# Local attention: six output tiles with the denominator's row inside them, and the copy of queries cut in four

## The reference

```python
s = jnp.einsum('bqgrd,bkgd->bgrqk', qblk, kb) * scale      # 128 queries against 256 keys
s = jnp.where(mask, s, NEG_INF)
pr = softmax(concatenate([s, sink]))[..., :-1]
o = einsum('bgrqk,bkgd->bqgrd', pr, vb) * silu(z)
```

## Time and profile before

| what | value |
|---|---|
| median of 3 runs | 3059.87 us (3055.61 to 3060.7) |
| the profiled execution | 3053.61 us, its span 3051.8 us |
| granted TensorE clock | 0.977 of full speed |
| PE busy | 2892.7 us, 95% |
| VectorE, ScalarE, GpSimd busy | 64%, 52%, 46% |
| the local attention, from its first maxima to its last output | 476.1 to 729.3 us of the span |

### The profile page before, as it was taken

One profiled execution on the slowest core, in us unless ns is written; L12 is line 12 of the kernel. 1 busy time (PEld: TensorE's weight loads), 2 busy tenths in 40 slices (PEclk: granted clock), 3 DMA queues, 4 the chain that ended last, 5 costly groups with the idle time before them and its releaser, 6 DMA issues. The chain is left out here.

```text
span 3051.8 us, 41224 instructions
## 1 busy us (share of the span) xinstructions
PE 2892.7 (95%) x13411; PEld 2328.4 (76%) x13411; DVE 1938.8 (64%) x3398; ACT 1590.5 (52%) x2808; POOL 1392.0 (46%) x1139
## 2 busy tenths in 40 slices
PE   8999996888999999999998799999999999899998
PEld 6888884566888788777877588888888878688776
DVE  4543315663578864555664588888888887357875
ACT  3111114666445544444544277777777777534643
POOL 0022104665232540001440388888888889423353
PEclk9999997999999999999999699999999999999999
DMA  5343437565997675455799634435335342498674
GB/s 165 84 136 125 117 118 242 179 203 172 308 277 239 201 247 183 159 177 167 251 328 380 148 73 102 103 73 116 91 78 127 73 92 87 157 301 270 212 243 145
DMA packets 284760, 530.13 MB, mean 174 GB/s; under 512 B 29200, under 2 KB 110992, under 8 KB 277392
## 3 DMA queue, kind: packets, MB, share of 16 engines
q1 hardware_dynamic: 218528, 391.22, 43.3%
q10 hardware_dynamic: 66032, 136.48, 14.7%
HBM read 346.85 MB, written 180.49 MB: 173 GB/s over the span
## 5 line engine op out<-in xcount | busy, mean ns | idle before, releaser
L2609 POOL TENSOR_TENSOR mla_pl<-mla_p,mla_ph 128x512 fp32r<-128x512 f32 (+3 forms) x640 | 702.9, 1121 | 144.4 <-ACT mla_p L2458 141.5
L1523 PE MATMUL end_bank<-end_xh,end_whi 128*128 128x512 f32 x1808 | 718.1, 397 | 44.3 <-DVE end_wlo L1754 17.0
L1525 PE MATMUL end_bank<-end_xh,end_wlo 128*128 128x512 f32 x1808 | 708.2, 392 | 0.0
L1524 PE MATMUL end_bank<-end_xl,end_whi 128*128 128x512 f32 x1808 | 707.6, 391 | 0.0
L1592 ACT CAST end_whi<-early_wraw 128x1024 fp32r<-128x1024 f32 (+1 forms) x204 | 211.4, 1036 | 531.8 <-PE end_bank L1525 510.7
L2457 ACT ACTIVATE mla_ph<-mla_score 128x512 fp32r<-128x512 f32 (+3 forms) x640 | 342.4, 535 | 238.0 <-PE mla_score L2285 232.9
L1754 DVE TENSOR_TENSOR end_wlo<-early_wraw,end_whi 128x1024 fp32r<-128x1024 f32 x188 | 255.4, 1358 | 317.9 <-ACT end_whi L1592 317.7
L1523 PEld LDWEIGHTS end_bank<-end_xh,end_whi 128*128 128x128 f32 x1808 | 342.1, 189 | 134.9 <-DVE end_wlo L1754 24.6
L2542 DVE TENSOR_TENSOR mla_acc<-mla_acc,mla_p 128x512 f32<-128x512 f32 (+3 forms) x576 | 351.0, 609 | 106.6 <-ACT mla_p L2458 104.2
L1524 PEld LDWEIGHTS end_bank<-end_xl,end_whi 128*128 128x128 f32 x1808 | 342.3, 189 | 72.6 <-issue 2.9
L1525 PEld LDWEIGHTS end_bank<-end_xh,end_wlo 128*128 128x128 f32 x1808 | 341.6, 189 | 72.4
(11 more groups left out here) (242 smaller groups left out, 4985.7 us busy)
## 6 DMA issues: line engine op xcount, KB each, us to landing
early_wraw<-in_pe_gate ACTq DMA_DIRECT2D x64, 512.0 KB, 4.9
early_wraw<-in_w_out ACTq DMA_DIRECT2D x62, 512.0 KB, 7.3
early_wraw<-in_w_in ACTq DMA_DIRECT2D x56, 512.0 KB, 3.8
scratch_q<-in_rope SPq DMA_DIRECT2D x64, 256.0 KB, 2.9
swa_q<-scratch_q SPq DMA_DIRECT2D x8, 2048.0 KB, 9.2
end_factor<-scratch_inv SPq DMA_DIRECT2D x64, 256.0 KB, 9.6
scratch_proj<-end_out_f SPq DMA_DIRECT2D x64, 256.0 KB, 6.9
scratch_sum<-end_out_f SPq DMA_DIRECT2D x64, 256.0 KB, 6.3
```

Source lines behind the costliest of these rows:

```text
L1523: nc.tensor.matmul(bank, wh[:, at], xh[:, k0 + k * nq, :], start=(k == 0), stop=False)
L1524: nc.tensor.matmul(bank, wh[:, at], xl[:, k0 + k * nq, :], start=False, stop=False)
L1525: last = nc.tensor.matmul(bank, wl[:, at], xh[:, k0 + k * nq, :], start=False, stop=(k == kc - 1))
L2609: pool.tensor_tensor(p_lo[b][:, off:TC], prob[b][:, off:TC], p_hi[b][:, off:TC].bitcast(F32), ALU.subtract).then_inc(p_lo_ok, 1)
```

## The change

The number of output tiles of the local attention goes from three to six (`n_out`), and each gets 65 rows in place of 64. The row of denominators, which had three tiles of its own, now lies in row 64 of the output tile of its chunk, so the memory taken stays the same. The semaphores `stored` and `den_stored` become six each. The copy of the queries, one instruction of 64x4096 at k=5, becomes four of 64x1024 at k=9, 10, 12 and 13. Each stands at the head of VectorE's list for its step; the one at k=9 comes before the joining of the maxima. PE waits for all four before the first scores of the next unit.

```diff
+        n_out = 3 if long else 6
...
-            den_row = [s.sb(f"den_row{b}", [1, TC]) for b in range(small)]
-        o_out = [s.sb(f"o_out{b}", [HEAD_DIM, TC]) for b in range(small)]
+        o_out = [s.sb(f"o_out{b}", [HEAD_DIM if long else HEAD_DIM + 1, TC]) for b in range(n_out)]
+        if not long:
+            den_row = [tile[HEAD_DIM:HEAD_DIM + 1, :] for tile in o_out]
...
-        stored, den_stored = ([s.sem(f"{n}{b}") for b in range(small)] for n in ("stored", "den_stored"))
+        stored = [s.sem(f"stored{b}") for b in range(n_out)]
+        den_stored = [s.sem(f"den_stored{b}") for b in range(n_out)]
...
-        copy_at = 5
+        copy_at = (9, 10, 12, 13)
+        q_parts = len(copy_at)
...
-                        pe.wait_ge(q_copied, u + 1)
+                        pe.wait_ge(q_copied, q_parts * (u + 1))
...
-                if c >= small:
-                    act.wait_ge(den_stored[c % small], 16 * (c // small))
-                act.copy(den_row[c % small][:], o_ps[c % 2][HEAD_DIM:HEAD_DIM + 1, :]).then_inc(row_ok, 1)
+                if c >= n_out:
+                    act.wait_ge(den_stored[c % n_out], 16 * (c // n_out))
+                act.copy(den_row[c % n_out], o_ps[c % 2][HEAD_DIM:HEAD_DIM + 1, :]).then_inc(row_ok, 1)
...
-            def copy_queries(u):
+            def copy_queries(u, part):
+                mine = slice(part * qw // q_parts, (part + 1) * qw // q_parts)
...
-                vec.tensor_copy(q_tiles[1][u % 2][0:HEAD_DIM, :], q_tiles[0][u % 3][0:HEAD_DIM, :].bitcast(F32)
+                vec.tensor_copy(q_tiles[1][u % 2][0:HEAD_DIM, mine], q_tiles[0][u % 3][0:HEAD_DIM, mine].bitcast(F32)
...
-                if c >= small:
-                    dve.wait_ge(stored[c % small], 16 * (c // small))
+                if c >= n_out:
+                    dve.wait_ge(stored[c % n_out], 16 * (c // n_out))
...
-                    if not long and k == copy_at and u + 1 < units:
-                        copy_queries(u + 1)
+                    if not long and k in copy_at and u + 1 < units:
+                        copy_queries(u + 1, copy_at.index(k))
```

More of the change, by code:

```diff
@@ L2115, in attention_phase @@
             den_turned, den_copied, dens_stored = s.sem("den_turned"), s.sem("den_copied"), s.sem("dens_stored")
-        else:
-            den_row = [s.sb(f"den_row{b}", [1, TC]) for b in range(small)]
         gate = [s.sb(f"gate{b}", [HEAD_DIM, TC]) for b in range(n_gate)]
-        o_out = [s.sb(f"o_out{b}", [HEAD_DIM, TC]) for b in range(small)]
+        o_out = [s.sb(f"o_out{b}", [HEAD_DIM if long else HEAD_DIM + 1, TC]) for b in range(n_out)]
+        if not long:
+            den_row = [tile[HEAD_DIM:HEAD_DIM + 1, :] for tile in o_out]
         if long:
@@ L2272, in _ @@
             cfg["next_loads"](sp)
-            for b in range(small):
-                sp.wait_ge(stored[b], 16 * len(range(b, len(chunks), small)))
+            for b in range(n_out):
+                sp.wait_ge(stored[b], 16 * len(range(b, len(chunks), n_out)))
                 if not long:
-                    sp.wait_ge(den_stored[b], 16 * len(range(b, len(chunks), small)))
+                    sp.wait_ge(den_stored[b], 16 * len(range(b, len(chunks), n_out)))
             if long:
@@ L2429, in store @@
                     act.wait_ge(row_ok, c + 1)
-                    act.dma_start(cfg["den_dst"](*chunks[c]), cfg["row"](den_row[c % small])
-                                  ).then_inc(den_stored[c % small], 16)
+                    act.dma_start(cfg["den_dst"](*chunks[c]), cfg["row"](den_row[c % n_out])
+                                  ).then_inc(den_stored[c % n_out], 16)
                 act.wait_ge(gated, c + 1)
-                act.dma_start(cfg["dst"](*chunks[c]), cfg["gate"](o_out[c % small])).then_inc(stored[c % small], 16)
+                act.dma_start(cfg["dst"](*chunks[c]), cfg["gate"](o_out[c % n_out][0:HEAD_DIM, :])).then_inc(stored[c % n_out], 16)
             def load_gate(c):
@@ L2561, in out_gate @@
                 dve.wait_ge(gate_in[c % n_gate], 16 * (c // n_gate + 1))
-                if c >= small:
-                    dve.wait_ge(stored[c % small], 16 * (c // small))
-                vec.tensor_tensor(o_out[c % small][:], o_ps[c % 2][0:HEAD_DIM, :], gate[c % n_gate][:], ALU.mult
+                if c >= n_out:
+                    dve.wait_ge(stored[c % n_out], 16 * (c // n_out))
+                vec.tensor_tensor(o_out[c % n_out][0:HEAD_DIM, :], o_ps[c % 2][0:HEAD_DIM, :], gate[c % n_gate][:], ALU.mult
                                   ).then_inc(gated, 1)
@@ L2571, in _ @@
             if not long:
-                copy_queries(0)
+                for part in range(q_parts):
+                    copy_queries(0, part)
             for g in range(total + tail):
@@ L2594, in out_gate @@
                 pool.wait_ge(gate_in[c % n_gate], 16 * (c // n_gate + 1))
-                if c >= small:
-                    pool.wait_ge(stored[c % small], 16 * (c // small))
-                pool.tensor_tensor(o_out[c % small][:], o_sum[c % 2][:], gate[c % n_gate][:], ALU.mult
+                if c >= n_out:
+                    pool.wait_ge(stored[c % n_out], 16 * (c // n_out))
+                pool.tensor_tensor(o_out[c % n_out][0:HEAD_DIM, :], o_sum[c % 2][:], gate[c % n_gate][:], ALU.mult
                                    ).then_inc(gated, 1)
```

## The result

| | before | after |
|---|---|---|
| median of 4 runs (lowest to highest), us | 3057.74 (3051.65 to 3060.7) | 3036.61 (3036.04 to 3038.42) |
| ratio, 95% interval | 1 | 0.9925 [0.9911, 0.9939] |
| profiled execution, us | 3053.6 | 3038.42 |
| first to last score matmul, us | 231.98 | 212.32 |
| lost beyond 1.87 or 1.40 a step, us | 33.5 | 13.8 |

The kernel before has one run more here than when I forecast. The ratio is 22.9 us of its median, 18.7 to 27.2 by its interval.

A forecast was written before the change was run, and what follows sets the result against it. PE was taken to set the phase's pace, with 33.5 us lost to waits. 12.3 + 1.6 + 4.3 + 1.2 - 8.4 - 0.2 = 10.8 us saved from 3059.9 gave 3049, range 3041 to 3058.

The forecast's parts named there:

- The copy comes to k=9 to 13: Unit's end: copy parts lock POOL out of the shared port, costing 1.2 us a unit, 8.4 in all (2.1 to 14).
- my own sum: Odd units, VectorE's list up to the gating for k=12: 4.6 us where about 3.2 are left, so PE stands 1.4.
- my budget of 11.6 - 9.8 - 0.45: POOL at k=9 to 15: 11.6 us needed, 9.8 in seven steps, 0.45 slack, so 1.3 us over.
- slower rival: Unit's end: POOL always slips in ahead of waiting VectorE, 3.6 us a unit, slower by 6, 3066; chance 0.08.
- The port costs almost nothing: Unit's end: joining gets the port first in even units, 0.3 us a unit remain, 17 saved, 3043; chance 0.2.
- k=10 term: Three odd units: gated output late behind maxima and copy, 2.4 us lost, half counted as saved; 0 or 2.4 open.
- late stores: Nine steps where VectorE waits for an output store: six tiles save 12.3 us, and 1.6 in the steps behind.
- PE's waits for the gated output: Profile sign: PE's waits for gated output fall from 13.7 us to about 8, mostly at k=11 to 13.
- The copy at k=5: In five units the query copy at k=5 delays POOL or the maxima; moving it away saves 4.3 us.
- losses at k=3: Three even units: gated output late because the unit's first chunk has one step only; 2.2 us, expected to stay.
- units' ends: Where ScalarE makes the sinks' exponentials and their store: 8.2 us lost in six units, expected to stay.
- gates rival: Gate loads, with 1 us to spare, take the stores' place as VectorE's wait: 1.8 us saved, 3058; chance 0.17.

The follow-up runs named there:

- e4: Changed kernel with the first two units' query copies made before the loop and none in it: ratio 0.9917, phase 211.09 us.
- e3: Changed kernel with one whole query copy at k=9 in place of four parts: ratio 0.9973, phase 225.29 us.
- e11: Changed kernel with each in-loop copy part preceded by a small 64x16 copy: ratio 0.9949, phase 220.99 us.
- e12: Changed kernel with the query copy in two halves, at k=9 and k=12: ratio 0.9942, phase 218.58 us.
- e1: Changed kernel with six output tiles but the query copy whole and at k=5 as before: ratio 0.9935, phase 216.71 us.
- e6: Changed kernel with each gate loaded one chunk ahead in place of two: ratio 0.9917, phase 212.10 us.
- e2: Changed kernel with the copy in four parts but three output tiles as before: ratio 0.9998, phase 232.99 us.
- e8: Changed kernel with ScalarE's store of the sinks' exponentials, and its wait, moved behind the exponentials of k=14: ratio 0.9910, phase 205.57 us.

## Why the prediction failed

**The step that failed is "The copy comes to k=9 to 13".** I took 1.2 us a unit, 8.4 in all, with bounds of 2.1 and 14. Taking the copies out gives back 1.2 us at most (e4), under my lower bound; the losses at k=11 and k=13 come to 0.95, and most of that the unit's end swallows. Two things went wrong in it.

First, in odd units I let POOL's next operation go between the joining and the second part. It happened in none of them. The second part asked 0.06 us before POOL did. In the even units I had left open who goes first, and the joining did, by 0.11 us; POOL's operation then ran between it and the second part, where nothing that PE wanted stood behind. Without that 1.28 us my own sum reads 4.6 - 1.3 = 3.3 for 3.2 left, and the lateness is nearly nil. I had set the value by two ways of counting that met near 1.2 to 1.4. They met by chance: the one had an operation of POOL too many in it, the other the whole time of all four parts, though they overlap POOL's idle time.

Second, I charged POOL 2.6 us for parts and joining. It was held for 1.44 in odd units and 0.83 in even ones, mostly because the first part lies in a gap of 0.59 us in which POOL waits for ScalarE. With 0.83 to 1.44 in place of 2.6, my budget of 11.6 - 9.8 - 0.45 comes out between -0.4 and 0.2 us a unit, and what remains falls into the unit's end, where ScalarE holds everybody up.

That the four parts fit is narrow. Two halves cost 6.3 us more, one piece 13.0, doubled parts 19.4, and small copies that move almost nothing 8.7. So the slower rival's mechanism is real, as e3, e11 and e12 show, but in the changed kernel the parts miss it by 0.06 us in odd and 0.11 us in even units. That the order fell so is luck: nothing in the kernel fixes it, and I hadn't counted to hundredths. "The port costs almost nothing", which I gave 0.2, was the case that came, at 3043; the time fell below it for the next reason and a rest.

**The k=10 term was halved without need.** I kept 1.2 of 2.4 us since the last gating would be 0.1 us early by my arithmetic. All of it went.

**What held.** The late stores: none is left in after, and 12.3 + 1.6 stays in the sum. The parts take 0.67 to 1.77 us and POOL's operations up to 1.78, as I had said. PE's waits for the gated output, forecast at about 8 us, came to 1.5. The copy at k=5 was worth about what I had said: e1 against after gives 4.4 us, where 4.3 + 2.4 less the 1.2 measured for the new place makes 5.5. The losses at k=3 (2.15 for 2.2) and at the units' ends stay (8.65 for 8.2). The first unit's copy took 2.48 us in four parts, 0.2 more than in one. No unit behind the first waited for a part at its first step. With the two terms corrected the sum is 12.3 + 1.6 + 4.3 + 2.4 - 1.2 - 0.2 = 19.2, against 19.7 measured in the phase.

**The gates rival was over-weighted.** I gave it 0.17 with "1 us to spare". Part of it came: the slowest gate went from 12.1 to 13.8 us, near the 14 that I had feared. But I had reckoned with 13 to 15 us for its eight steps; VectorE gated with that one 17.4 us after its issue, 3.6 us after its landing, and e6 runs with six steps.

**Open.** The runs say 18.7 to 27.2 us, the phase 19.7. The rest lies within the interval and within the 4 us by which the phase's start varies, and no run here separates them. e2 shows besides that the terms don't add: -1.0 and 15.3 alone, 19.7 together. Work taken off an engine that waits for a landing lengthens its wait, which was 18.5 us before and 25.2 in e2.

## What to carry to other kernels

A write buffer's depth is read from the slowest landing in the busiest stretch, divided by the step there: 11.6 us over 1.87 is more than six steps, and with tiles for four, six and ten steps VectorE waited 18.5, 5.4 and 0 us for stores. An operation that locks a port costs its neighbour next to nothing where it lies in a gap that the neighbour has anyway, so cut it to the length of these gaps. Price the order in which both ask for the port from the timeline, instant by instant, not as a sum of durations: for each request, note when the data of the neighbour's next operation are ready. Before you rely on such a fit, double the suspect: the four parts cost at most 1.2 us and twice the parts 19.4 more, which tells how near the edge the fit is.

## What the runs showed of the hardware

- Who asks first for the shared port gets it next. I take the start of a row as its request, since the row of an operation that is held is longer by the wait. In the 14 profiles a copy or a joining on VectorE and an operation of POOL overlap 502 times (by more than 0.1 us), and each time the one whose row starts first also ends first, even where it leads by 0.01 us (543.77 against 543.78 in e11). The later one waits until the other's operation is over, whatever its own size: 1.31 us for the 64x16 copy that takes 0.16 alone. The Trainium skill, in "SBUF — State Buffer", section "Who interferes with whom", says that whoever issues first has the pair for the whole instruction and the other fully blocks; these rows agree.
- A wait and a store in ScalarE's own list hold back the exponentials behind them: moving the sinks' store and the wait for it by two steps (e8) shortened the phase by 212.32 - 205.57 = 6.75 us and left every computation as it was. 5.5 of it lie at k=14 and 15.
- A store of 128 KB lands in 2.4 us where little else moves (86 GB/s in 692 to 706 us). The one issued at 555.5 before took 11.4, the one at 557.0 after 11.6, where all queues together moved 336 GB/s in 557 to 568 us. The slowest of the phase took 11.6 before and 12.8 after. Six tiles hide that, they don't shorten it.
